# Moving copies, gate-tile reloads, the own-key chain and the first K-page requests in a hybrid attention and MoE step

## The reference

```python
h = rms_norm(x, norm1) * (1 + scale1) + shift1
q, k, v, logf, gates = project_in(h, w_in, b_f)       # gates: sigmoid, (rows, 3 branches, 1024)
(o_sb, o_dil, o_fox), state = mix_fn(q, k, v, logf)   # prompt rows: on themselves; sample rows: on 2048 past keys
merged = (gates[:, :, 0] * (o_sb  @ w_br_sb)
        + gates[:, :, 1] * (o_dil @ w_br_dil)
        + gates[:, :, 2] * (o_fox @ w_br_fox))
x = x + gate1 * (merged @ w_o)
h2 = rms_norm(x, norm2) * (1 + scale2) + shift2
x = x + gate2 * hier_moe(h2, ...)                     # 16 experts, top 2 of one group of 4
# state, sample rows: new_bufs.append(ctx[:, t:])     # each window buffer, moved on by 4 rows
```

## Time and profile before

| | |
|---|---|
| median of 3 runs | 1552.7 us (1549.16 to 1556.25) |
| the profiled execution, its own time | 1555.62 us |
| its span, first to last instruction | 1553.6 us |
| mean granted TensorE clock | 0.902 of full speed |
| busy: PE, DVE, ACT, POOL | 1268.4, 451.1, 296.7, 160.9 us |
| bytes moved | 304.23 MB, mean 196 GB/s |

### The profile page before, as it was taken

One profiled execution on the slowest core, in us unless ns is written; L12 is line 12 of the kernel. 1 busy time (PEld: TensorE's weight loads), 2 busy tenths in 40 slices (PEclk: granted clock), 3 DMA queues, 4 the chain that ended last, 5 costly groups with the idle time before them and its releaser, 6 DMA issues.

```text
span 1553.6 us, 20055 instructions
## 1 busy us (share of the span) xinstructions
PE 1268.4 (82%) x6991; PEld 828.4 (53%) x6991; DVE 451.1 (29%) x1106; ACT 296.7 (19%) x613; POOL 160.9 (10%) x229
## 2 busy tenths in 40 slices
PE   3699999656699999957888888874995799999990
PEld 2377776433477777744555555553644444444440
DVE  4200000654212223223444443433445111111116
ACT  2200001322122122112222222211210111111112
POOL 0000000400111112200000000000000121111110
PEclk9899999777799999977898898877997799999995
DMA  8733332259522221079887888657001999999934
GB/s 309 263 108 110 111 108 100 81 180 332 187 81 63 88 77 56 12 271 313 281 274 251 266 286 291 234 199 259 26 31 36 336 334 318 309 313 331 312 122 172
DMA packets 152741, 304.23 MB, mean 196 GB/s; under 512 B 16014, under 2 KB 79271, under 8 KB 150176
## 3 DMA queue, kind: packets, MB, share of 16 engines
q1 hardware_dynamic: 143264, 281.55, 53.9%
q0 software_dynamic: 9408, 21.82, 3.8%
HBM read 283.37 MB, written 50.00 MB: 215 GB/s over the span
## 4 chain that ended last, share of the span: by engine, by line
PE 75%; DVE 10%; issue 4%; DMA 4%; SPq 4%; ACT 2%; another core or an unknown queue 1%; POOL 0%; DVEq 0%; POOLq 0%; ACTq 0%
PE psum L841 64%; PE psum L1124 6%; DVE arena L1720 3%; DMA wring<-in_w_mod 2%; PE psum L1163 2%; PE psum L1388 1%; DVE wring L1728 1%; SPq L628 1%; DVE hT L2300 1%; PE psum L1052 1%; PE psum L970 1%; DVE wring L1720 1%; DVE arena L1728 1%; DVE xT L2091 1%
## 5 line engine op out<-in xcount | busy, mean ns | idle before, releaser
L841 PE MATMUL psum<-hT,wring 128*128 128x272 f32 x1280 | 303.9, 396 | 8.3 <-ACT hT L1445 8.3
L841 PEld LDWEIGHTS psum<-hT,wring 128*128 128x128 f32 x1280 | 241.2, 191 | 68.8 <-issue 20.8
L841 PE MATMUL psum<-arena 128*8 128x128 f32 (+6 forms) x1488 | 207.6, 338 | 6.6 <-DVE arena L1720 3.5
L841 PE MATMUL psum<-wring,hT 128*128 128x512 f32 x384 | 173.0, 604 | 17.5 <-DVE hT L2300 15.4
L841 PEld LDWEIGHTS psum<-arena 128*8 128x8 f32 (+5 forms) x1488 | 109.9, 119 | 92.7 <-issue 78.3
L841 PE MATMUL psum<-wring,arena 128*8 128x128 f32 (+3 forms) x1008 | 118.2, 411 | 19.6 <-DMA wring<-in_w_mod 14.0
L841 PEld LDWEIGHTS psum<-wring,hT 128*128 128x128 f32 x384 | 71.8, 192 | 104.8 <-issue 101.8
L841 PEld LDWEIGHTS psum<-wring,arena 128*8 128x8 f32 (+3 forms) x1008 | 51.9, 111 | 74.2 <-issue 60.4
L841 PE MATMUL psum<-arena,small 128*128 128x256 f32 (+8 forms) x162 | 51.5, 442 | 39.7 <-DVE arena L1720 27.7
L1124 PE MATMUL psum<-small,arena 128*128 128x128 f32 x392 | 65.3, 322 | 20.8 <-DMA arena<-in_cache_kv 13.1
L779 POOL TENSOR_SCALAR wring<-wring,arena 128x384 f32<-128x384 f32 (+6 forms) x32 | 45.7, 1427 | 292.0 <-DVE arena L1939 292.0
(11 more groups left out here) (236 smaller groups left out, 1207.7 us busy)
## 6 DMA issues: line engine op xcount, KB each, us to landing
wring<-in_w SPq DMA_DIRECT2D x48, 1024.0 KB, 11.2
arena<-in_cache_kv SPq DMA_DIRECT2D x128, 320.0 KB, 3.5
wring<-in_w_mod SPq DMA_DIRECT2D x12, 2048.0 KB, 13.4
arena<-in_w SPq DMA_DIRECT2D x24, 1024.0 KB, 5.0
xT<-in_cache_kv SPq DMA_DIRECT2D x64, 320.0 KB, 3.5
wring<-in_cache_kv SPq DMA_DIRECT2D x64, 320.0 KB, 3.6
out_dil_sample<-in_cache_dil SPq DMA_DIRECT2D x8, 2044.0 KB, 37.0
wring<-in_w_in SPq DMA_DIRECT2D x6, 2048.0 KB, 11.8
```

What stands on the lines that cost most here:

```text
L841: return T.matmul(out, lhsT, rhs, start=start, stop=stop, **k)
```

## The change

Four edits, and the places of memory that they need.

- **Shift copies.** The 16 copies of the two small windows stay ahead of the gate weights. The 8 copies of 2 MB are asked for between the gate-weight loads: two behind load 0, one behind each of loads 2 to 7.
- **Own-key chain.** Its instructions are placed inside the attention steps: the scores ahead of unit 0, the rest at steps 1 to 6. Its products go to PSUM bank 5 instead of banks 0 and 1.
- **First K pages.** SP waits for the scores of all units and asks for pages 0 to 3 of sequence 0; the waits for the end of attention (`attention_done`) stand ahead of page 4.
- **Gate tiles.** Six batches of four instead of five of five, in a ring of two batches in `hT`. SP asks for batches 0 and 1 behind the last page; ACT asks for batches 2 to 5, each when the sigmoids of the batch that lay there are done. `x1p` is asked for behind `w_o`; `x1s` lies in the ring's place and waits for 20 sigmoids.

```diff
+            for b in range(NB):
+                shift_copy(0, b)
+                shift_copy(1, b)
             sp.wait_ge(sem("st_k"), 16 * KV_STORES)
             for c in range(GATES // 2):
                 if c == 1:
+                    for b in range(2):
+                        shift_copy(2, b)
                     sp.wait_ge(sem("sbo_mm"), 4)
                 if c >= 3:
                     sp.wait_ge(sem("gate_mm"), 4 * (c - 2))
                 sp.dma_start(gate_w[c % 3], ...)
+                if 2 <= c < NB:
+                    shift_copy(2, c)
                 if c >= 4 and c % 2 == 0:
                     gate_store(c // 2 - 2)
             gate_store(4)
             gate_store(5)
-            for n in range(2):
-                sp.wait_ge(sem(f"st_g{n}"), 16 * 3)
-            gate_load(0)
-            sp.wait_ge(sem("pv_mm"), NU)
-            ... (the other waits, now in attention_done)
...
+                    if b0 == 0 and p == 4:
+                        attention_done()
                     page(b0, p, 0, kpage[p % 8], f"ld_k{p % 8 // 2}", free)
...
+            sp.wait_ge(sem("sc_mm"), nsub)
+            sp.wait_ge(sem("qbd_ready"), 1)
+            sp.wait_ge(sem("ld_pt"), 32)
             sequence(0, 0)
...
             sequence(0, NB - 1)
+            for n in range(2):
+                sp.dma_start(gate_in[:, STAGE * n:STAGE * n + STAGE, :], gate_d[...]).then_inc(sem(f"st_g{n}"), 16)
...
-            sp.dma_start(x1p, ...)
...
-            gate_load(1)
             for half in range(2):
                 chunk(30 + half, half, wo[:, 512 * half:512 * half + 512])
+            sp.dma_start(x1p, ...)
...
+            sp.wait_ge(sem("gate_ev"), 2 * GATES + 5 * STAGE)
             sp.dma_start(x1s[0:32, :], ...)
-            for n in range(2, 5):
-                sp.wait_ge(sem("gate_ev"), 2 * GATES + TURN * (n - 1))
-                gate_load(n)
```

On PE, with `own_scores` and `own_after` new (64 products of 4 rows by 8 columns, and one of 4 by 128):

```diff
             pe.wait_ge(sem("nck_ev"), NFOX)
+            own_scores()
             for n in range(NU):
+                if n == 2:
+                    own_after()
+                if n == 5:
+                    pe.wait_ge(*done_at("new_t"))
                 if n + 2 < NU:
                     scores(n + 2)
```

On ACT, in the branch stage:

```diff
             for n in range(GATES):
...
-                f(gsig[:, n % 2, :], gate_in[n // TURN % 2][:, n % TURN, :], ACT.Sigmoid).then_inc(sem("gate_ev"), 1)
+                f(gsig[:, n % 2, :], gate_in[:, at, :], ACT.Sigmoid).then_inc(sem("gate_ev"), 1)
+                if n % STAGE == STAGE - 1 and turn < 4:
+                    act.wait_ge(sem("gate_ev"), 2 * GATES + n + 1)
+                    act.dma_start(gate_in[:, at + 1 - STAGE:at + 1, :], gate_d[:, n + 1 + STAGE:n + 1 + 2 * STAGE, :]
+                                  ).then_inc(sem(f"st_g{turn % 2}"), 16)
```

More of the change, by code:

```diff
@@ L500, in _, with shift_copy @@
                         sp.dma_start(dst, rows[:, 256 + 128 * g:384 + 128 * g]).then_inc(sem("st_smp"), 16)
-            for g in range(3):
+            def shift_copy(g, b):
                 W = DILATION[g] * 128
                 n = (W - NT) * 256
[L505 to L509, removed]
+                src = I[f"cache_dil{g + 1}"][b, 0].rearrange("w a h d -> (w a h d)")[1024:1024 + n]
+                dst = O[f"dil{g + 1}_sample"][b, 0].rearrange("w a h d -> (w a h d)")[0:n]
+                sp.dma_start(dst.rearrange("(s n) -> s n", s=16),
+                             src.rearrange("(s n) -> s n", s=16)).then_inc(sem("shift"), 16)
             def gate_store(n):
@@ L601, in _ @@
             sequence(0, NB - 1)
+            for n in range(2):
+                sp.dma_start(gate_in[:, STAGE * n:STAGE * n + STAGE, :], gate_d[:, STAGE * n:STAGE * n + STAGE, :]
+                             ).then_inc(sem(f"st_g{n}"), 16)
             sp.wait_ge(sem("kT_mm"), 18 * NB)
             sp.wait_ge(sem("qk_mm"), 5 * NB)
-            sp.dma_start(x1p, I["x_prompt"][0].rearrange("(i p) d -> p i d", p=P)).then_inc(sem("ld_tail"), 16)
             sp.wait_ge(sem("seq_pv"), NB - 1)
@@ L1068, in weigh, with own_scores, own_after @@
                 last.then_inc(sem("pv_mm"), 1)
+            def own_scores():
+                pe.wait_ge(sem("qbd_ready"), 1)
+                for b in range(NB):
+                    for j in range(8):
+                        tile = PAIR_TILES[j] if j < 5 else j - 3
+                        last = mm(banks[5][0:NT, 64 * b + 8 * j:64 * b + 8 * j + 8],
+                                  zT[:, 8 + tile, SEQ + NT * b:SEQ + NT * b + NT], qbd[:, b, 8 * j:8 * j + 8])
+                last.then_inc(sem("own_keys"), 1)
+            def own_after():
+                pe.wait_ge(*done_at("spn_ready"))
+                mm(banks[5][0:NT, 0:128], later_key[0:NT, 0:NT], spnew[:, :, :].rearrange("p b n -> p (b n)")
+                   ).then_inc(sem("own_keys"), 1)
             scores(0)
@@ L1082, in _ @@
             weigh(NU - 1)
-            pe.wait_ge(sem("qbd_ready"), 1)
-            pe.wait_ge(sem("sc_ev"), nsub)
-            for b in range(NB):
-                for j in range(8):
-                    tile = PAIR_TILES[j] if j < 5 else j - 3
-                    last = mm(banks[0][0:NT, 64 * b + 8 * j:64 * b + 8 * j + 8],
-                              zT[:, 8 + tile, SEQ + NT * b:SEQ + NT * b + NT], qbd[:, b, 8 * j:8 * j + 8])
-            last.then_inc(sem("own_keys"), 1)
-            pe.wait_ge(*done_at("spn_ready"))
-            mm(banks[1][0:NT, 0:128], later_key[0:NT, 0:NT], spnew[:, :, :].rearrange("p b n -> p (b n)")
-               ).then_inc(sem("own_keys"), 1)
             pe.wait_ge(*done_at("new_ready"))
@@ L1561, in _ @@
             for n, u in enumerate(units):
+                if n == 1:
+                    own_logs()
+                if n == 5:
+                    own_weights()
                 if n + 2 < NU:
```

114 lines of the change are left out of this document (63 added, 51 removed).

## The result

The changed kernel takes **1505.2 us** (median of 4 runs, 1503.1 to 1507.9) against 1554.0 (4 runs, 1549.2 to 1556.3): ratio 0.969, 95% interval 0.966 to 0.972. The prediction said 1529, with a range of 1510 to 1535, so the gain is twice the forecast one, 48.8 us against 23.5. Two later sets of runs of the same two kernels gave 1511.4 against 1550.4 (ratio 0.974, 0.971 to 0.977) and 1509.5 against 1552.9 (0.971, 0.968 to 0.974), so 39 to 49 us is what the change gives.

A forecast was written before the change was run, and what follows sets the result against it. The prediction took three gaps of PE, at 390, 665 and 1059 us, as the time the change can move. Gains of 7.9 + 11.0 + 4.6 = 23.5 us gave 1529 us, range 1510 to 1535.

The forecast's parts named there:

- Gap C: Branch stage at 1059 us, ACT idle 21.49 us before tile 10's sigmoid, waiting for gate tiles: gain of 4.6 us.
- at 1055.5 SP stands in L628: Branch stage: ACT's request behind tile 7 is held with SP's own, so tile 8 waits until 1073.3.
- ACT's requests are free: Rival for the branch stage: nothing holds ACT's requests, gain there 19.8 us, time 1514; chance 0.32.
- Gap A: At 390 us, a 13.47 us wait for gate weights standing behind the shift copies: gain of 7.9 us, 6.2 to 9.5.
- Gap B: At 665 us, between attention's end and the first page turning: everything moves 11.0 us earlier, 9.5 to 12.
- the case of B going wrong: Sign at the first K pages: page 4's request comes more than 5 us behind page 0's.
- That holds to the end of the sequences: The 11.0 us shift lasts through the sequences, since the 256 page requests run at SP's own pace.
- The sum: Whole kernel: 7.9 + 11.0 + 4.6 = 23.5 us gained, time 1529.
- The slower rival: Ring in `hT`, cover for four tiles only: four reloads each held 16.08 us, time 1577; chance 0.03.

The follow-up runs named there:

- router loads early: Changed kernel with the router's four small loads asked for during the attention steps instead of in the branch stage: 1512.4 us.
- router loads by ACT: Changed kernel with the requests for w_rg and w_re made by ACT behind its reload after tile 7, instead of by SP: 1528.3 us.

## Why the prediction was wrong

**Gap C, the step that failed.** "at 1055.5 SP stands in L628", so ACT's request would be held as SP's own was, 4.6 us in place of 19.8. ACT's four requests took 0.33 us each, three of them inside SP's 30.19 us. I priced an unknown by the rows nearest in place and time, L618 and L628, which are rows of another queue. The row that pointed the right way was one that I had: POOL issued four requests in 2.11 us from 9.80 while SP was held. (Not all four lie in the 3.17 us that I quoted, which end at 11.11; the last two run into SP's next request, held for 7.96 us from 11.14.) I set it aside, since POOL's is another kind of queue, and gave it 0.32. The branch stage gained 20.7 us on average (102.0 in the five profiles with the old reloads, 81.3 in the three of after), so the rival "ACT's requests are free", with 19.8, was right to a microsecond for this stage. That close a hit is in part luck: it said 1 us for a batch in cover, where batches 4 and 5 cost ACT 12.7 us; PE's lead over ACT, up to four tiles, hid most of them. The reading of gap C was incomplete as well: I put L628's 16.08 us down to a backlog of some 9 MB, but without the 2048 small rows the same backlog held no request of SP's for more than 5.4 us (router loads early, router loads by ACT). The rule of the Trainium skill that I weighed, in Perfetto Trace Analysis, section "DMA Instruction — HWDGE (DVE, Sync)", a shared generator that is locked while one sequencer uses it, would have ACT held behind SP; the measurements on this chip speak against that for requests from ACT and SP. The other one, DMA: Bandwidth & Descriptors, section "Queues, rings and completion order", turns between queues packet by packet, fits: batch 2 landed in 9.2 us (1016.18 to 1025.35), though `w_o`, `x1p` and the first modulation rows, some 8 MB, had been asked for by SP in the 7 us before it.

**Gap A, a size.** The mechanism held: no wait, own scores ahead of the unit. The first gate unit came 11.1 us earlier (mean of four profiles with the old copies 406.3, of nine with the new order and own scores 395.2) where I had 8.5 ahead of the unit. The own scores cost 3.36 us, not 5.0: I let them stretch with the clock, and they don't. The rest is that the wait itself scatters up to 4 us above the 13.47 that one profile showed. The 0.58 us inside the steps left no trace: first unit to first page shortened by 11.3 us on average, with it included.

**Gap B, right but for half a microsecond.** The first page's request came 1.32 us behind the end of the last store's (forecast 1.2) and the page was turned at 656.66 (forecast 657). Page 4's request came 5.79 us behind page 0's instead of 4.81, which by my own mark is the case of B going wrong; but what was lost lies ahead of it, between the first request and the first turning, 5.35 us instead of 4.79. In this pair of profiles 11.0 became 10.5.

**"That holds to the end of the sequences", right on average.** The 12.9 us of the first pair were scatter of the pages, between 327 and 340 us for either kernel. The lengths go with the granted clock (0.91 in the shortest, 0.86 in three of the four longest), but whether the clock sets the length, and what makes it fall and come back, is open; products added at the sequence's start did not hold it up. I had taken one profile's span for the kernel's.

**The sum.** With the means: 11.1 + 11.3 + 0.8 (pages) + 20.7 - 1.8 (behind the stage) = 42.1 us, against 39, 43 and 49 measured. Of the 18.6 that my 23.5 lack, C has 16.1; the first set of times, 1505.2, was the lowest of three. The slower rival, a ring of two that starves, was never near. A starving ring can be made, though it stays faster than before: asked for by SP the reloads cost 20.7 us, and behind 2048 small rows in ACT's own queue 18.8.

## What to carry to other kernels

Here requests of ACT's passed freely beside one of SP's that was held, and the long holds came with many small rows in the same queue. So price a request by what its own queue has undone, small rows first, and ask for a transfer that someone waits for at the moment when its buffer comes free; here that was done from the queue of the engine that frees it. Send loads of many small rows in a quiet stretch and nothing urgent behind them on the same queue. And take a second profile of the kernel before, before an account of two traces is closed: one stage's scatter (12 us here) can be as large as a part of the change.

## What the hardware did that I had not expected

- Products with 8 columns cost the same at both levels of the clock: 64 of them, x128 in the rows, took 3.36 us at 0.50 and at 1.00.
- Two requests for 80 KB in 2048 rows: 0.67 and 1.29 us in a quiet stretch, 0.52 and 30.19 us behind SP's backlog; and on ACT they took 0.56 and 3.20 us, and the request behind them was held for 14.86 us.
- PE's clock stayed at 0.50 through 12 us without a gap (838 to 850 us), in the kernel with added products.
- The same eight sequences, with the same instructions, take 327 to 340 us.
